# A second home for the first gate part of the second block's experts, loops per expert, and a last unit with moved gathers and combinations

## What is computed

```python
def moe_swiglu(h, router, wg, wu, wd):
    t = h.reshape(B * L, D)                       # 512 x 1024
    vals, idx = lax.top_k((t @ router).astype(jnp.float32), TOP_K)      # 2 of 8 experts
    gates = jax.nn.softmax(vals, axis=-1)
    combine = jnp.sum(jax.nn.one_hot(idx, N_EXPERTS_2) * gates[..., None], 1)
    for e in range(N_EXPERTS_2):
        out = out + combine[:, e:e + 1] * swiglu(t, wg[e], wu[e], wd[e])
    return out
...
        h = layer_norm(ALPHA * h + f, ln2_g[i], ln2_b[i])               # f: the experts' sum
```

## Time and profile before

| | us |
|---|---|
| median of 3 runs (3228.75 to 3231.43) | 3231.21 |
| the profiled execution | 3231.08 |
| its span in the trace | 3229.2 |
| PE busy in it | 2990.9 (93%) |
| mean granted TensorE clock | 0.959 of full |

### The profile page before, as it was taken

How to read it: one execution, slowest core, us unless ns; L and a number is a source line. 1 busy time by engine, 2 the same in 40 slices (tenths; PEclk the granted TensorE clock), 3 DMA queues, 4 the chain that set the end, 5 groups by cost and what they waited for, 6 DMA issues and landing times. The chain is left out here.

```text
span 3229.2 us, 43786 instructions
## 1 busy us (share of the span) xinstructions
PE 2990.9 (93%) x18418; PEld 1848.2 (57%) x18418; DVE 1048.4 (32%) x1946; ACT 548.7 (17%) x1262; POOL 220.9 (7%) x204
## 2 busy tenths in 40 slices
PE   8998899999789979989999999999999799999897
PEld 4544787654343338867578884478776444444343
DVE  5666665553311234631300002119212311010004
ACT  3222333221111121133000000011240000000001
POOL 0001321340000000011000000000010100000000
PEclk9999899999889989999999999999999799999998
DMA  3411000115389921202012142012120615547917
GB/s 115 107 52 43 4 16 29 40 48 237 139 340 430 418 89 70 86 21 118 0 52 78 68 166 78 0 68 74 61 81 13 248 50 223 215 171 322 417 48 292
DMA packets 79477, 414.03 MB, mean 128 GB/s; under 512 B 10675, under 2 KB 16179, under 8 KB 63588
## 3 DMA queue, kind: packets, MB, share of 16 engines
q1 hardware_dynamic: 68028, 384.75, 30.0%
q10 hardware_dynamic: 7848, 14.61, 1.8%
q0 software_dynamic: 3456, 12.58, 1.1%
HBM read 383.17 MB, written 28.76 MB: 128 GB/s over the span
## 5 line engine op out<-in xcount | busy, mean ns | idle before, releaser
L3312 PE MATMUL pgu<-gu,xg 128*64 128x320 f32 (+1 forms) x2560 | 393.5, 463 | 8.9 <-POOLq L3240 8.9
L2887 PE MATMUL pp<-feat,lead 128*128 128x264 f32 x1408 | 315.9, 388 | 2.0 <-DVEq L2901 2.0
L3312 PEld LDWEIGHTS pgu<-gu,xg 128*64 128x64 f32 x2560 | 182.3, 137 | 204.8 <-issue 130.4
L2887 PEld LDWEIGHTS pp<-feat,lead 128*128 128x128 f32 x1408 | 269.1, 191 | 48.6 <-DVEq L2901 2.2
L312 PE MATMUL proj<-feat,w 128*128 128x512 f32 x576 | 256.0, 598 | 2.6 <-PEq L153 2.6
L2465 PE MATMUL ring<-feat,lead 128*128 128x264 f32 x1024 | 244.6, 400 | 3.0 <-PEq L2912 1.5
L2465 PEld LDWEIGHTS ring<-feat,lead 128*128 128x128 f32 x1024 | 200.6, 198 | 42.6 <-issue 7.0
L3319 PE MATMUL py<-down,hm_t 128*64 128x512 f32 x880 | 200.3, 603 | 10.5 <-POOLq L3240 10.5
L2465 PE MATMUL ring<-feat,w 128*128 128x264 f32 x896 | 208.1, 390 | 0.0
L2465 PEld LDWEIGHTS ring<-feat,w 128*128 128x128 f32 x896 | 169.8, 192 | 31.5 <-issue 3.1
L312 PEld LDWEIGHTS proj<-feat,w 128*128 128x128 f32 x576 | 107.4, 191 | 124.8 <-issue 124.8
(11 more groups left out here) (493 smaller groups left out, 3488.1 us busy)
## 6 DMA issues: line engine op xcount, KB each, us to landing
gu<-in_moe_gu SPq DMA_DIRECT2D x16, 3072.0 KB, 10.0
gu<-in_moe_gu SPq DMA_DIRECT2D x16, 2560.0 KB, 15.7
ring<-in_w_gate SPq DMA_DIRECT2D x16, 2048.0 KB, 13.3
ring<-in_w_up SPq DMA_DIRECT2D x16, 2048.0 KB, 15.0
ring<-in_w_down SPq DMA_DIRECT2D x16, 2048.0 KB, 17.2
w<-in_w_in SPq DMA_DIRECT2D x15, 2048.0 KB, 7.8
down<-in_moe_down SPq DMA_DIRECT2D x8, 3072.0 KB
lead<-in_ffn_up SPq DMA_DIRECT2D x22, 1024.0 KB, 4.8
```

The costliest lines, as they stand in the source:

```text
L2887: last = pe.matmul(pp[:, b, a, half, 0:HALF], w[:, b, a, k * P:(k + 1) * P], core.feat[:, k, half * HALF:(half + 1) * HALF], start=k == 0, ...
L3312: last = pe.matmul(pgu[half(h), part, 0:n], xg[:, k, :], w[:, k, h, :], start=k == 0, stop=k == DK - 1)
```

## The change

- `gu` is made larger by one part (24 KB in each partition). Part 0 of an odd expert has its home at the front, everything else lies behind it (`gu_at`). Several tiles (`share`, `first`, `share_t`, `xg`, `sg`, `hm`, `hm_t`, `y`) move into `core.feat`, which is free by then; the order listings call them `feat`.
- SP loads part 0 one expert ahead: e1's part 0 right behind e0's last part, and in the pass for expert e first parts 1 to 5 of e, each when its home is free, then part 0 of e + 1. An odd expert's part 0 has a count of its own (`odd_landed`).
- PE and POOL run one loop per expert in place of one loop over all units, since the address of part 0 and the semaphore depend on the expert. Each reads the running total of units from `units` ahead of each loop (`units_until`). PE's last unit is a pass of the eighth loop, so it turns a next unit's rows like the others, which nothing reads. ACT and DVE keep their loop and their last unit.
- `share` is turned in `route_top_two` (PE, 8 calls, then a copy by DVE), no longer in the last unit.
- `got` lies over the even home of part 0 and the front of part 1. Only the two gathers of tile 3 wait for the last unit's `part_done[1]`; the others need `all_stored` alone.
- DVE's last unit runs `combine(0)` between the first copy of `hm_t` and `multiply(1)`, and `combine(1)` to `combine(3)` ahead of the copy of `y`. Before, `combine(0)` and `(1)` stood behind the unit, and `(2)` and `(3)` behind the copy.

```diff
+def gu_at(e, part):
+    return 0 if part == 0 and e % 2 else GU_AT[1] + GU_AT[part]
...
-        self.gu = core.sb(ctx, "gu", [P, GU_WIDTH])
+        self.gu = core.sb(ctx, "gu", [P, GU_WIDTH + GU_AT[1]])
...
+    def arrival(self, e, part):
+        if part:
+            return self.landed[part], 16 * (e + 1)
+        return self.odd_landed if e % 2 else self.landed[0], 16 * (e // 2 + 1)
...
                 last.then_inc(weights.first_turned, 1)
+                pe.wait_ge(weights.shared, 1)
+                for h in range(2):
+                    for t in range(TILES):
+                        last = pe.matmul(pt[h * UT:(h + 1) * UT, t * P:(t + 1) * P], weights.share[:, t, :], ident, start=True, stop=True)
+                last.then_inc(weights.share_turned, 1)
...
                 do(weights.features(dve, px))
+                dve.wait_ge(weights.share_turned, 1)
+                do(dve.tensor_copy(weights.share_t[:, :], pt[:, :]))
...
-        got = gu[:, 0:2 * TILES * D].rearrange("p (t a d) -> p t a d", t=TILES, a=2)
+        got = gu[:, GU_AT[1]:GU_AT[1] + 2 * TILES * D].rearrange("p (t a d) -> p t a d", t=TILES, a=2)
...
                 for part in range(2, PARTS):
                     weights.load(sp, 0, part)
+                weights.load(sp, 1, 0)
                 for e in range(1, NX):
-                    before = sp.value_load(units[0:1, UNITS + e:UNITS + e + 1], min_val=1, max_val=UNITS)
-                    for part in range(PARTS):
+                    before = units_until(sp, e)
+                    for part in range(1, PARTS):
                         sp.wait_ge(part_done[part], before)
                         weights.load(sp, e, part)
+                    if e + 1 < NX:
+                        sp.wait_ge(part_done[0], before)
+                        weights.load(sp, e + 1, 0)
...
-                with pool.Fori(0, unit_count(pool)) as s:
-                    e = pool.value_load(units[0:1, bass.ds(s, 1)], min_val=0, max_val=NX - 1)
-                    for part in range(PARTS):
-                        pool.wait_ge(weights.landed[part], e * 16 + 16)
-                        pool.sem_inc(part_ready[part], 1)
+                begin = 0
+                for e in range(NX):
+                    end = units_until(pool, e + 1)
+                    with pool.Fori(begin, end):
+                        for part in range(PARTS):
+                            landed, count = weights.arrival(e, part)
+                            pool.wait_ge(landed, count)
+                            pool.sem_inc(part_ready[part], 1)
+                    begin = end
                 pool.wait_ge(all_stored, 1)
-                last = last_unit(pool)
-                for part in range(2):
-                    pool.wait_ge(part_done[part], last + 1)
-                    pool.sem_inc(got_free, 1)
-                pool.wait_ge(got_free, 2)
                 for t in range(TILES):
+                    if t == TILES - 1:
+                        pool.wait_ge(part_done[1], units_until(pool, NX))
+                        pool.sem_inc(got_free, 1)
+                        pool.wait_ge(got_free, 1)
...
-                last = last_unit(pe)
-                with pe.Fori(0, last) as s:
-                    unit(s)
-                unit(last, final=True)
-                pe.wait_ge(share_out, 1)
-                pe.wait_ge(y_out, last + 2)
+                begin = 0
+                for e in range(NX):
+                    end = units_until(pe, e + 1)
+                    with pe.Fori(begin, end) as s:
+                        unit(s, e)
+                    begin = end
+                pe.wait_ge(y_out, end + 1)
...
                     dve.tensor_copy(hm_t[:, 0:6, :].rearrange("p c t -> p (c t)"), pt[:, 0, 0:3 * P]).then_inc(hm_out, 1)
+                    if final:
+                        dve.wait_ge(enlarged, TILES + 1)
+                        combine(0)
                     multiply(1)
-                    dve.wait_ge(turned, s + 2)
-                    if final:
-                        dve.tensor_copy(share_t[:, :], px[:, :]).then_inc(share_out, 1)
-                    else:
+                    if not final:
+                        dve.wait_ge(turned, s + 2)
                         weights.features(dve, px).then_inc(xg_out, 1)
...
                 unit(last, final=True)
-                dve.wait_ge(enlarged, TILES + 1)
-                combine(0)
-                combine(1)
+                for t in range(1, TILES):
+                    combine(t)
                 rows_out(last)
-                combine(2)
-                combine(3)
```

57 lines of the change are left out of this document (27 added, 30 removed).

## The result

| | before | changed |
|---|---|---|
| median of 16 runs each | 3232.12 us | 3241.39 us |
| lowest to highest | 3228.75 to 3236.62 | 3235.95 to 3244.77 |
| profiled execution, its time | 3231.1 us | 3241.38 us |
| its span | 3229.2 us | 3239.6 us |

The ratio is 1.0024, with a 95% interval from 1.0017 to 1.0032. I had predicted 3230.6 us (3225.5 to 3237.5), so the sign and the range are both wrong. The interval leaves 1 out: the changed kernel is slower, by 0.24%.

A forecast was written before the change was run, and what follows sets the result against it. It took DMA to bound u12 to u15, PE the other units, DVE the stretch behind 3201; 1.3 - 2.4 + 0 + 0.5 = -0.6 us gave 3230.6 us, with 8 in 10 within 3225.5 to 3237.5.

The forecast's parts named there:

- The start, +1.3: Routing's end up to u1: turning `share` there delays e0's parts 2 to 5, so u1 starts 1.3 us later.
- both matmul terms: At the start: the 16 matmuls that turn `share` start within 1.3 us, and the last takes 0.27 us.
- the 0.3 us for the overlap: At the start: 0.3 us subtracted from the delay of the routing's end, for the overlap of PE's pipelined end.
- The DMA-bound stretch, -2.4: u12 to u16: early part 0 saves 7.7 us, the stream starts 5.25 us later; u16 starts 2.4 us earlier.
- The boundaries, 0: Seven boundaries between experts: PE's count load (0.48 us) and about 0.3 us more hide behind covers of 5.8 us.
- The wait for `hm` itself stays: First units of experts: the wait, 1.58 us in u4, stays as before; 0.5 us either way for each of five.
- Rival B: Entering new code costs at four boundaries: +7 us (3237.6) at 7.5 us per load, +31 at 13.5; chance 0.09.
- two statements of the Trainium skill: PE's branches back: every one pays beyond two pages of 256 instructions, or none with room for 2048; trace favours the second.
- Last unit and tail, +0.5: u19 to the end: combinations leave the tail, but `combine(0)` ahead of `multiply(1)` stalls PE 4.5 us, plus 2.6 slower matmuls.

The follow-up runs named there:

- the second pair: The changed kernel and the kernel before, each executed again unchanged for a second profile: 3240.88 us (ratio 1.0020) and 3232.24 us (ratio 1.0001).
- e9: The changed kernel with PE's eight loops folded into one loop over pairs of experts, code for two unit bodies: 3237.63 us, ratio 1.0011 to the kernel before.

## Why the prediction was wrong

**The start, +1.3: mis-sized.** Measured +2.5 (52.3 to 54.8), and +3.0 in the second pair. The cost of 16 matmuls was taken from a row of u19, where the granted clock is 1.00, for a place where PE runs at the lower level: from 2543 to 2557 us of the trace of before it is 0.50. With both matmul terms doubled my own sum would have been 2.6 + 0.5 - 0.3 = 2.8 (the 0.3 us for the overlap stands in no row).

**The DMA-bound stretch, -2.4: right for the home, but not the net.** The home gives 2.1 to 2.2 us, as worked out; code packets, counted at nothing, take 1.5 back. What is left, -0.6 us, is the size of the scatter between two executions, so in the first comparison the gain seemed not to exist.

**The boundaries, 0: right on PE.** No execution shows a PE gap at the head of u4, u8, u11 or u13 in the changed kernel.

**"The wait for `hm` itself stays": the step that failed, with the code's transfers put at nothing.** I allowed 0.5 us either way for each wait for `hm`, as the weights in flight are the same. They grew by 0.65 us in u4 and 1.0 in u11. I looked for the price of code on PE, where it is fetched and hidden, and not at the engines that move it. The earlier trace rows held the hint: code comes as packets over the DMA engines on its first pass, and the store that ACT waits for runs on the same engines under load. And I had no bound for the clock, which turned 0.65 us of wait into 2.34. Rival B had the cause, new code, but the wrong victim (PE's sequencer) and a price of 7.5 us per load; what came was 2.4 and 2.7 us at two of four boundaries.

The prediction also cites two statements of the Trainium skill and reads the trace of before as agreeing with the second (room for 2048 instructions) against the first (a window of two pages). That trace left it open: a unit shows 381 of PE's instructions, fewer than the 512 of two pages. What bears on it is e9: two bodies, entered in turn, and no code packet from u5 to the tail.

**Last unit and tail, +0.5: right in its mechanism.** Measured -0.4 in the first pair and +0.5 in the second. The first gather came 20.0 us behind u19's first matmul (forecast 19.9), `combine(0)` 26.4 us (forecast 26.5). PE's wait was 5.36 us (forecast 4.5) and 6.49 in the second execution, and the slower matmuls behind it cost 1.7 us, not 2.6. Undoing the part freed 3.0 us, which my sum had not asked for: it compared the change with before, not with the gathers alone.

In sum, the forecast was -0.6 and the profiles show +7.2. The 7.8 us between them are 1.2 from the start, 4.7 from u4, u8 and u11, 2.8 from the stretch u12 to u16 (a gain of 2.4 forecast, 0.4 longer in this pair), less 0.9 in the tail.

## What to carry to other kernels

Where a small store runs among large loads, do not wait for it ahead of work that does not need it: moving one wait behind one Silu gave 5 us, more than the whole change was to give. Unrolled loops cost DMA packets, not only room, and whoever waits for a transfer of many shares at that moment pays; a loop over pairs keeps alternating buffers with code for two bodies. Taking a wait away gains nothing while another one ends later: the gathers stood behind the relay of the last weights, 1.0 to 1.8 us behind their landing in every execution, and not behind the parts that they overwrite. And take a duration only from a row at the clock of the place where the work will stand.

## What the runs showed of the hardware

- One 16 KB packet of PE's code that comes during another engine's store makes that store late: 14.2 us in place of 13.5, with PE itself not held up. 140 increments of a semaphore in the instruction stream ahead moved the packets by 11 to 13 us within their units, and the delay with them.
- A store of 128 packets of 2 KB took 13.5 us beside loads in packets of 20 and 24 KB, 9.5 us beside loads in packets of half that size, and landed 2.3 us behind its issue with no loads in flight.
- Behind a wait of 1.58 us the granted clock stayed at 1.00, behind 2.23 and 2.58 us it was 0.73 and 0.76 for 6 to 7 us. Of the 14 waits for `hm` of 2.19 us or more in u4, u8 and u11, 12 cost 1.5 us or more beyond the wait itself and two (2.25 and 2.51 us) did not; one of 1.76 us did (u8 with one home, 33.9 us), none up to 1.7 us. The length of the wait is thus not all that decides.
- With 50 increments of a semaphore on TensorE's queue the gap ahead of the next matmul was 6.2 and 7.2 us, in place of 1.4 and 3.1: by an estimate from these gaps, 0.12 to 0.14 us each if nothing else fills them.
